# First expert block's rows by matrix products instead of through DRAM, and the turning of the rows ahead of the down product, in one inference step of a four-layer mixture-of-experts trunk

## What is computed

```
def moe(h, w_router, router_bias, w_gate, w_up, w_down):
    s = sigmoid(h @ w_router)                  # 16 experts in 4 groups
    sb = s + router_bias
    ...                                        # best group, then the top 2 experts inside it
    gates = sum(one_hot(idx) * w)              # w: the two scores, normalised to sum 1
    a = einsum('bsd,edf->bsef', h, w_gate)     # d = 1024, f = 256
    u = einsum('bsd,edf->bsef', h, w_up)
    act = silu(a) * u * gates
    return einsum('bsef,efd->bsd', act, w_down)
```

## Time and profile before

| what | value |
|---|---|
| device time, median of 3 runs | 1914.86 us (1914.83 to 1915.51) |
| device time of the profiled execution | 1910.18 us |
| span of the profiled execution on the trace | 1908.4 us |
| PE busy | 1479.9 us (78% of the span) |
| DVE, ACT, POOL busy | 26%, 20%, 12% of the span |
| mean granted clock of PE | 0.911 of full speed |
| bytes moved by DMA | 446.88 MB, mean 234 GB/s |

### The profile page before, as it was taken

The page is one execution under the profiler, slowest core; times in us unless marked ns, Lnnn a source line. Parts: engine busy times, 40 slices in busy tenths (PEclk is TensorE's granted clock), DMA queues, the critical chain, the costliest instruction groups (busy, mean ns, idle before and its releaser), DMA issues.

```text
span 1908.4 us, 26946 instructions
## 1 busy us (share of the span) xinstructions
PE 1479.9 (78%) x11269; PEld 900.8 (47%) x11269; DVE 496.5 (26%) x1105; ACT 385.2 (20%) x983; POOL 234.0 (12%) x296
## 2 busy tenths in 40 slices
PE   2999975997495893899378989849983988849990
PEld 1776752333384672333174456623332766733330
DVE  0126321111326513111223342221113055131113
ACT  1115221111212602111111342201112035011111
POOL 1030012000115012000101000110002030210001
PEclk8999997999698997999789999979996999969995
DMA  9696265998476064699828213649985740538963
GB/s 351 254 327 164 81 256 197 392 415 320 179 257 180 7 243 171 246 419 379 304 90 288 66 45 111 270 157 391 412 324 204 250 118 1 208 145 326 420 280 121
DMA packets 129282, 446.88 MB, mean 234 GB/s; under 512 B 13011, under 2 KB 54822, under 8 KB 104582
## 3 DMA queue, kind: packets, MB, share of 16 engines
q1 hardware_dynamic: 97206, 351.37, 48.8%
q0 software_dynamic: 25152, 89.96, 13.6%
q10 hardware_dynamic: 6800, 3.78, 0.6%
HBM read 395.38 MB, written 49.69 MB: 233 GB/s over the span
## 4 chain that ended last, share of the span: by engine, by line
PE 71%; DVE 10%; issue 7%; DMA 6%; ACT 3%; POOL 1%; SPq 0%; POOLq 0%; DVEq 0%; ACTq 0%
PE bank L1395 62%; PE bank L1693 3%; DMA y_slots<-kT 3%; PE bank L1545 3%; PE bank L1451 2%; DVE pp L1311 2%; DMA xn<-y_slots,row_of 2%; DMA ring<-in_w_mod 1%; DVE xn L1016 1%; ACT pp L898 1%; POOL small L581 1%; DVE V L1372 1%; DVE V L1374 1%; DVE x L1375 1%; PE bank L1589 1%
## 5 line engine op out<-in xcount | busy, mean ns | idle before, releaser
L1395 PE MATMUL bank<-ring,pp 128*32 128x512 f32 x2784 | 417.0, 595 | 17.3 <-DVE pp L1311 14.6
L1395 PE MATMUL bank<-work,pp 128*32 128x512 f32 x1056 | 280.2, 598 | 8.3 <-DVE pp L1311 8.3
L1395 PE MATMUL bank<-ring,hT 128*128 128x256 f32 (+3 forms) x1142 | 262.7, 390 | 6.9 <-DVE hT L1027 3.2
L1395 PEld LDWEIGHTS bank<-ring,hT 128*128 128x128 f32 x1142 | 208.2, 191 | 59.3 <-issue 27.1
L1395 PEld LDWEIGHTS bank<-ring,pp 128*32 128x32 f32 x2784 | 126.8, 110 | 171.7 <-issue 171.7
L1395 PE MATMUL bank<-ring,xn 128*128 128x256 f32 x768 | 169.2, 381 | 0.0
L1395 PE MATMUL bank<-V,pp 128*32 128x512 f32 x768 | 148.8, 619 | 12.3 <-DVE pp L1311 12.3
L1395 PEld LDWEIGHTS bank<-ring,xn 128*128 128x128 f32 x768 | 144.8, 190 | 23.0 <-issue 3.7
L1451 PE MATMUL bank<-ident,xn 128*128 128x128 f32 x192 | 39.5, 397 | 130.3 <-DVE xn L1016 130.3
L1327 DVE TENSOR_TENSOR pp<-bank,pp 128x256 f32<-128x256 f32 x48 | 20.4, 425 | 398.9 <-ACT pp L970 398.9
L1395 PEld LDWEIGHTS bank<-work,pp 128*32 128x32 f32 x1056 | 76.6, 111 | 86.1 <-issue 86.1
(11 more groups left out here) (216 smaller groups left out, 1524.3 us busy)
## 6 DMA issues: line engine op xcount, KB each, us to landing
ring<-in_w_mod SPq DMA_DIRECT2D x96, 1024.0 KB, 9.1
ring<-in_moe_w_down SPq DMA_DIRECT2D x52, 1024.0 KB, 14.4
ring<-in_moe_w_gate SPq DMA_DIRECT2D x32, 1024.0 KB, 16.6
ring<-in_moe_w_up SPq DMA_DIRECT2D x32, 1024.0 KB, 8.5
hT<-h_slots POOLq DMA_DIRECT2D x48, 512.0 KB, 11.1
y_slots<-kT POOLq DMA_DIRECT2D x48, 512.0 KB, 8.3
V<-in_moe_w_gate SPq DMA_DIRECT2D x16, 1024.0 KB, 8.8
V<-in_moe_w_up SPq DMA_DIRECT2D x16, 1024.0 KB, 12.1
```

The source lines that it names most:

```text
L1395: return pe.matmul(out, lhsT, rhs, start=start, stop=stop)
```

## The change

A new constant `slot_no` holds the numbers 0 to 127 on every partition; it is an eighteenth small load. Behind `row_of`, DVE builds `first_of`, three 128x128 matrices of zeros and ones, which lie in a part of `kT` that is not yet in use: element (token, slot) is 1 if either of the token's two slot numbers is that slot. It takes three comparisons and three compare-and-adds. PE multiplies the rows `xn` with them in `gather_rows` (24 float32 products of 128 columns, which is 48 records) and so makes the turned rows of block 0 directly in banks 6 and 7; the copies out of the banks are as before. The scatter to `h_slots` stays, all six DMAs of it; the read of block 0 from the table goes, and the reads of blocks 1 and 2 need wait for nothing but the scatter. In PE's stream `turn_rows(blk + 1)` moves in front of `block_down(blk - 1)`, and in those of ACT and DVE the copies of turned rows move in front of the copies of the down product. The placement of the adaLN products between the output projections is as it was.

The core of the diff, without the lines of constants and semaphores:

```
                 def block_in(blk):
-                    if blk >= 2:
+                    if blk > 2:
                         pool.wait_ge(xT_full, BLOCKS * L + blk - 1)
...
-                block_in(0)
                 block_in(1)
...
                 V_.tensor_copy(row_of[:, :, :], row_f[:, :, :]).then_inc(rows_ready, 1)
+                for b in range(NB):
+                    last = V_.tensor_scalar(first_of[:, b, :], slot_no[:, :], row_f[:, 0, b:b + 1], None, ALU.is_equal)
+                link(last)
+                for b in range(NB):
+                    last = V_.scalar_tensor_tensor(out=first_of[:, b, :], in0=slot_no[:, :],
+                                                   scalar=row_f[:, 1, b:b + 1], in1=first_of[:, b, :],
+                                                   op0=ALU.is_equal, op1=ALU.add)
+                last.then_inc(first_ready, 1)
...
+                def gather_rows(n):
+                    pe.wait_ge(first_ready, L + 1)
+                    pe.wait_ge(xT_a, n + 1)
+                    pe.wait_ge(xT_v, n + 1)
+                    wait_evacuated(pe, *[("hrow", L, b, half) for b in range(NB) for half in range(2)])
+                    for k in range(KC):
+                        for b in range(NB):
+                            ins = mm(bank[6 + k // 4][:, k % 4 * P:(k % 4 + 1) * P], xn[:, b, k::KC],
+                                     first_of[:, b, :], b == 0, b == NB - 1)
+                    ins.then_inc(xT_full, 1)
...
-                turn_rows(BLOCKS * L, 0, 16 * (BLOCKS // 2 * L + 1))
+                gather_rows(BLOCKS * L)
                 for blk in range(BLOCKS):
                     n, slot = BLOCKS * L + blk, blk % 2
                     block_gate_up(blk)
+                    if blk < BLOCKS - 1:
+                        turn_rows(n + 1, 1 - slot, loaded(blk + 1))
                     if blk > 0:
                         block_down(blk - 1)
-                    if blk < BLOCKS - 1:
-                        turn_rows(n + 1, 1 - slot, 16 * (BLOCKS // 2 * L + (blk + 1) // 2 + 1))
```

More of the change, by code:

```diff
@@ L60, in host_constants @@
                rope32=rope(32).reshape(P, 64), first=first,
-               before=r < c, quarters=r % 32 == np.arange(E)[None], ebase=np.tile(SLOTS * np.arange(E)[None], (P, 1)),
+               before=r < c, slot_no=np.tile(np.arange(P)[None], (P, 1)), quarters=r % 32 == np.arange(E)[None], ebase=np.tile(SLOTS * np.arange(E)[None], (P, 1)),
                ebeyond=np.tile(E * SLOTS + (FURTHER - SLOTS) * np.arange(E)[None] - SLOTS, (P, 1)),
@@ L244, in build @@
         quarters = sb("quarters", [P, E])
+        slot_no = sb("slot_no", [P, P])
         rbias = sb("rbias", [P, E])
@@ L326, in build @@
              "r_copied"))
-        lat_sq, lat_rstd, states, wr_ready = (sem(s) for s in ("lat_sq", "lat_rstd", "states", "wr_ready"))
+        lat_sq, lat_rstd, states, wr_ready, first_ready = (sem(s) for s in ("lat_sq", "lat_rstd", "states", "wr_ready", "first_ready"))
         freed = {"v": freed_v, "a": freed_a, "p": probs, "w": wo_mul}
@@ L970, in _ @@
                     nc.scalar.activation(sil[:, slot, :], bank[slot][:, 0:DE], ACT.Silu).then_inc(sil_full, 1)
+                    if blk < BLOCKS - 1:
+                        turned_rows(n + 1, 1 - slot)
                     if blk > 0:
                         first_half(blk - 1)
-                    if blk < BLOCKS - 1:
-                        turned_rows(n + 1, 1 - slot)
                     turn_act(act, n, slot)
@@ L1035, in _ @@
                 free(V_.tensor_copy(dst, src.rearrange("p (c k) -> p c k", c=2) if n == 16 else src))
-            dve.wait_ge(const_in, 16 * 17)
+            dve.wait_ge(const_in, 16 * 18)
             for w in range(2):
@@ L1435, in _ @@
             mods([("mod", 0, v, q) for v in range(2) for q in range(4)])
-            pe.wait_ge(const_in, 16 * 17)
+            pe.wait_ge(const_in, 16 * 18)
             def mod_columns(L, s):
@@ L1754, in block_down, with loaded @@
                     ins.then_inc(y_full, 1)
[L1756 removed]
+                def loaded(blk):
+                    return 16 * (BLOCKS // 2 * L + blk // 2 + 1 if blk % 2 else (BLOCKS // 2 - 1) * L + blk // 2)
+                def gather_rows(n):
[9 more added lines that the diff above has]
+                gather_rows(BLOCKS * L)
                 for blk in range(BLOCKS):
```

5 lines of the change are left out of this document (3 added, 2 removed).

## The result

| what | before | after |
|---|---|---|
| device time, median (4 runs each) | 1914.84 us (1912.26 to 1915.51) | 1868.84 us (1865.95 to 1870.13) |
| ratio, with its 95% interval | | 0.976 (0.9743 to 0.9777) |
| profiled execution, its span | 1910.18, 1908.4 us | 1865.95, 1864.2 us |
| mean granted clock of PE | 0.911 | 0.927 |

The change made the kernel 46.0 us faster. The forecast was 70 us faster, 1845 us, and the range ended at 1860: the direction was right, the size was not, and the time lies 9 us outside the range. In the two profiled executions the difference is 44.2 us of span.

The account below looks back on a forecast made before the run. The prediction took PE to set the pace, with the transfers having almost no room. Four layers saving 10.2 us at the mixture's start and 7.3 in the blocks made 70 us, giving 1845 us, range 1828 to 1860.

Parts of the forecast that it names:

- near block 9: Late in a mixture stage: one PE wait of 1 to 2 us for a weight transfer, once the period is 11.7 us.
- The forecast's balance: Expert 13's weights at gate-up 9: 5.8 - 7.0 + 1.1 - 1.4 = -1.5 us, so PE waits 1.5 us a stage.
- the transfers set every block: Rival, blocks: transfers hold the period at 12.6 us, only the starts' 41 us remain, 1874 us; chance 0.09.
- the read of block 1: Start of each mixture: issued 12.7 us after PE's last count, landing at 16.3, before the first gate-up ends at 18.0.
- gather 7.9 us: Start of each mixture: 48 records, 19.5 in 4.4 us at low clock, the rest in 3.5; bounds 6.0 and 10.8.
- a gather above 11 us: Sign at the start of each mixture that would show the forecast wrong; about 8 us was expected.
- With the clock up: First gate-up product of each mixture: 7.1 us with its tail, instead of 9.0, after the gather.
- first_ready: Start of each mixture: DVE's six instructions take 1.5 us, so it comes 2.0 us after PE's last count.
- The same instructions remain: Blocks: PE's 10.43 + 1.00 + 0.25 = 11.7 us a period without wait, 0.88 less than 12.58.
- The serial gather: Rival, start of each mixture: a record's load and product do not overlap, gather 13.3 us, 1867 us; chance 0.04.
- The late clock: Rival, start of each mixture: clock stays down through the gather, saving 7.3 us there, 58 in all, 1856; chance 0.11.
- No rows came late: Refers to the slower rival, blocks: late reads stop turning and down product, landing after 19.7 us, 1921 us; chance 0.03.

Follow-up runs that it names:

- run 12: Not a run label: in "the blocks, which now run 12 us earlier", "run" is a verb and 12 us a time.

## Why a record of the gather costs 0.244 us

The forecast took the price from weight loads of 128x128 that stood in a row, 0.125 us at full clock and 0.225 at half. Those loads read neighbouring columns. The gather's stationary operand is `xn[:, b, k::KC]`, every eighth float, 32 bytes apart. The next experiments change how these 128 columns lie. The prices of single records below are distances between the starts of neighbouring records in the trace, layer 0.

**Neighbouring columns.** The edit multiplies other columns of `xn` (the result is another one); count, shapes and order of the records stay.

```diff
-                            ins = mm(bank[6 + k // 4][:, k % 4 * P:(k % 4 + 1) * P], xn[:, b, k::KC],
+                            ins = mm(bank[6 + k // 4][:, k % 4 * P:(k % 4 + 1) * P], xn[:, b, k * P:(k + 1) * P],
```

> The changed kernel, but gather_rows reads 128 neighbouring columns of xn as its stationary operand instead of every eighth column. Leaves out the right choice of columns: block 0 then multiplies the wrong 128 features with each part of the weights, with the same instructions and sizes. Theory A (the strided read of float32 weights sets the 0.244 us a record): the gather takes 6.0 to 8.5 us instead of 11.7, first gate-up product ends 3 to 5.5 us earlier in each layer, 1847 to 1857 us in all. Theory B (load and product of a record simply follow one another, or three accumulations into one place do): 11.7 us as before and 1869 us.

Measured: 1852.05 us (1851.4 to 1853.37), ratio 0.9692 (0.9676 to 0.9708). The gather takes 8.10, 8.15, 8.55 and 7.27 us in the four layers; the forecast was 7.9. Chain of layer 0, then three stretches of its gather, columns as above:

```profile
290.08 8.10 PE bank L1404 x48
...
299.14 7.11 PE bank L1404 x64
```

```profile
291.00:295.00 4.00, 4.00 (x21) 4.00 (x20) 1.83 (x10) 0.00 (x0) 3.08 (x4) 0.50 0.91 360
294.00:295.00 1.00, 1.00 (x7) 1.00 (x6) 0.00 (x0) 0.00 (x0) 0.69 (x2) 0.50 0.99 401
296.00:298.00 2.00, 2.00 (x20) 1.97 (x18) 0.00 (x0) 0.00 (x0) 0.94 (x1) 1.00 0.96 377
```

Here the records do follow the clock: they start 0.213 us apart at half clock and 0.111 at full, where those of the changed kernel start 0.240 and 0.238 apart. So the stride costs 0.03 us a record while the clock is low and 0.13 once it is up: what it takes away is the gain from the clock.

**Steps of 8 and of 16 bytes**, to see where the price begins:

```diff
-                            ins = mm(bank[6 + k // 4][:, k % 4 * P:(k % 4 + 1) * P], xn[:, b, k::KC],
+                            ins = mm(bank[6 + k // 4][:, k % 4 * P:(k % 4 + 1) * P], xn[:, b, k % 4 * 2 * P:(k % 4 + 1) * 2 * P:2],
...
-                            ins = mm(bank[6 + k // 4][:, k % 4 * P:(k % 4 + 1) * P], xn[:, b, k::KC],
+                            ins = mm(bank[6 + k // 4][:, k % 4 * P:(k % 4 + 1) * P], xn[:, b, k % 2 * 4 * P:(k % 2 + 1) * 4 * P:4],
```

> The changed kernel, but gather_rows reads every second column of xn as its stationary operand, not every eighth; block 0 then multiplies the wrong 128 features with each part of the weights. Theory A (any step between the columns of a float32 product's weights doubles their read): 0.244 us a record, 11.7 us, as with a step of eight. Theory B (the price grows with the step, or comes from where the eight-fold step lands in memory): a gather between 8 and 11 us.

> The changed kernel, but gather_rows reads every fourth column of xn as its stationary operand (16 bytes apart; eight-fold steps are 32 bytes, two-fold 8); block 0 then multiplies the wrong 128 features with each part of the weights. With steps of one and two the gather took 8.1 to 8.3 us in layer 0, with eight 11.73 whatever the clock. Theory A (the price grows with the distance): 9 to 10.5 us in layer 0. Theory B (there is a bound at 32 bytes): 7.3 to 8.5. Theory C (the bound lies at 16): 11.7.

Measured, one run each: 1853.43 us with step two, and gathers of 8.18, 8.29, 7.29 and 7.59 us; 1869.48 us with step four, and 11.45 us in every layer. The chains of both, step two first:

```profile
290.40 8.18 PE bank L1404 x48
```

```profile
291.81 11.45 PE bank L1404 x48
```

| step, bytes | a record at half clock, us | at full clock, us | gather, layer 0, us |
|---|---|---|---|
| 4 | 0.213 | 0.111 | 8.10 |
| 8 | 0.213 | 0.118 | 8.18 |
| 16 | 0.233 | 0.233 | 11.45 |
| 32 | 0.240 | 0.238 | 11.73 |

Every second float is all but free, every fourth costs nearly what every eighth does, whatever the clock. These four steps fit a price that depends on how many of the floats read lie in 16 bytes: with two or more it is hardly seen, with one the read sets the pace. They don't tell this from a bound on the step itself between 8 and 16 bytes. The Trainium skill states such a rule ("Advanced Engine Details and Errata", section "Memory Cachelines"): the buffer has lines of 16 bytes and wants at least two hits on one. The runs agree with it. The Trainium skill ("SBUF — State Buffer", the note on cachelines in the section "Door 1: The DMA port swizzle") puts the free stride at four floats; step four at 11.45 us against 8.18 speaks against this, and the measurement decides. Why 32 bytes cost a little more than 16, and 8 a little more than 4, stays open.

**The same product from rows that are stored permuted.** The float of index 8j + k is put at 128k + j when the rows are copied out of PSUM, so that the gather and the transposes read neighbours and nothing else is computed. The copies now write with a step of 512 bytes.

```diff
-                return xn[:, key[2], key[3] * 512:(key[3] + 1) * 512], ps[:, :]
+                return (xn[:, key[2], :].rearrange("p (k j) -> p j k", k=KC)[:, key[3] * 64:(key[3] + 1) * 64, :],
+                        ps[:, :].rearrange("p (j k) -> p j k", k=KC))
...
-                                           xg[:, slot, k::KC], ident[:, :])
+                                           xg[:, slot, k * P:(k + 1) * P], ident[:, :])
...
-                            ins = mm(bank[6 + k // 4][:, k % 4 * P:(k % 4 + 1) * P], xn[:, b, k::KC],
+                            ins = mm(bank[6 + k // 4][:, k % 4 * P:(k % 4 + 1) * P], xn[:, b, k * P:(k + 1) * P],
```

> The changed kernel with the features of every row stored in another order (8 j + k at place 128 k + j), so that gather_rows and turn_rows read neighbouring columns; the copies of hrow out of PSUM write in steps of 512 bytes instead. Same result. Theory A (the strided read of float32 weights is the gather's cost): the gather takes 7.3 to 8.6 us, as in the run with neighbouring columns, and the time is within 4 us of that run's 1852. If the strided writes of the six hrow copies cost more than the reads gain, the copies (0.59 and 0.69 us now) take well over 1 us each and PE's last count comes later by up to 3 us a layer: over 1860. The transposes, 0.125 us each with a stride, should not change by more than 0.02 each.

Measured: 1853.52 us (1850.03 to 1859.58), ratio 0.9688 (0.9671 to 0.9704), gathers of 8.56, 7.72, 8.28 and 8.46 us. The copy of the rows in the timeline of the changed kernel, and then in this one:

```profile
276.04 0.69 DVE L1012 COPY xn<-bank 128x512 f32<-128x512 f32 x1 [2.87 <-PE bank L1668]
```

```profile
277.33 1.04 DVE L1013 COPY xn<-bank 128x512 f32<-128x512 f32 x1 [2.91 <-PE bank L1669]
```

The scattered write costs 0.35 us a copy on DVE (and 0.47 on ACT), ahead of a gather that is some 3.5 us shorter. Against the kernel before in its own set of runs, this kernel is 58.2 us faster and the one with neighbouring columns 58.7, the changed kernel 46.0 and 42.7. So what neighbouring columns give, some 12 to 16 us, can be had without computing something else.

**The clock's share.** In the third layer the first gate-up took 8.75 us, not 7.11. The stretch 1239 to 1241 of the changed kernel:

```profile
1239.00:1241.00 2.00, 2.00 (x12) 0.46 (x8) 0.00 (x0) 0.00 (x0) 0.54 (x1) 0.50 0.93 297
```

The clock was back at 1.2 GHz there, although PE had been busy for the 11.7 us of the gather up to a pause of 1 us for the copies. Of the 28 stages in the seven profiled runs with a gather of 11.4 us or more, 9 had a first gate-up of 8.6 to 8.8 us; of the 20 stages in the five runs with a gather of 7.1 to 8.6 us none had. In three of those 20 the clock fell one pause later instead, ahead of the second gate-up (8.7 to 8.8 us where 7.07 is usual). In all nine the clock had risen 5.47 to 6.23 us after the gather began, in the other 19 at most 5.45 or at least 6.50 us after; so when it rises has to do with whether it falls again. Why it falls in one stage and not in the next was not settled.

## Why the period is 12.10 us and not 11.7

The sum of the forecast was 10.43 + 1.00 + 0.25. The rows after read 7.00 + 3.57 = 10.57 for the same products, 1.09 for the eight transposes and 0.44 for the two. Before, gate-up and down ran into each other and the two transposes stood in front of a wait; now products and transposes change places four times in a period instead of twice. Two experiments take the added changes back in different ways, and the 0.75 us wait does not return.

**All transposes in a row**, ahead of the down product. ACT's copy of the turned activations moves ahead of its copy of the down product too; PE's stream:

```diff
                     if blk < BLOCKS - 1:
                         turn_rows(n + 1, 1 - slot, loaded(blk + 1))
-                    if blk > 0:
-                        block_down(blk - 1)
                     pe.wait_ge(act_full, n + 3)
                     pe.wait_ge(acT_ready, n + 1)
                     turn_gated(act_sb[:, slot, :]).then_inc(acT_full, 1)
+                    if blk > 0:
+                        block_down(blk - 1)
```

> The changed kernel with the two transposes of the gated activations moved right behind the eight of the rows, ahead of the down product. Theory A (changes between products and transposes cost 0.13 us each): two changes fewer in a period, 11.8 to 11.9 us instead of 12.10, 4 x 10 x 0.25 = 10 us less, 1858 to 1860. Theory B (the transfers hold the period near 12.1, or bring waits once the period is shorter): the period on PE shows waits for weights and the time is 1864 to 1869. If SiLU and DVE's product are not done when the eight transposes end, PE waits 0.1 to 0.4 us a period for DVE and the gain is half or less.

Measured: 1872.81 us (1870.07 to 1878.39), ratio 0.9797 (0.978 to 0.9813). The timeline of PE shows why it gives nothing: its 96 records of products take 10.48 us (10.57 in the changed kernel), but SiLU and DVE's product have only the eight transposes as cover, and PE stands 0.20 us for them; the last block, which turns no rows, has no cover at all, and PE stands 1.30 us. The blocks of a stage take 135.1 us instead of 132.9.

```profile
369.92 1.16 PE L1702 MATMUL bank<-ident,hT 128*128 128x128 f32 x8
371.29 0.51 PE L1714 MATMUL bank<-ident,pp 128*128 128x128 f32 x2 [0.20 <-DVE pp L1336]
...
444.08 0.51 PE L1714 MATMUL bank<-ident,pp 128*128 128x128 f32 x2 [1.30 <-DVE pp L1336]
```

**All transposes in a row, in the middle of the down product**, whose first half then covers SiLU. ACT's copy of the turned activations moves as in the experiment before; of `block_down`, which now takes the halves it is to do, only the calls are shown:

```diff
                     block_gate_up(blk)
+                    if blk > 0:
+                        block_down(blk - 1, (0,))
                     if blk < BLOCKS - 1:
                         turn_rows(n + 1, 1 - slot, loaded(blk + 1))
-                    if blk > 0:
-                        block_down(blk - 1)
...
                     turn_gated(act_sb[:, slot, :]).then_inc(acT_full, 1)
+                    if blk > 0:
+                        block_down(blk - 1, (1,))
```

> The changed kernel with both groups of transposes between the two halves of the down product, so that one half stands directly behind the gate-up product and the other directly ahead of the next. Theory A (a change between products and transposes costs PE some 0.13 us each, and this leaves two of four): SiLU's result, ready 1.35 us behind the gate-up product, is there before the transposes ask for it, and a period takes 11.8 to 11.9 us; about 10 us less in all, 1857 to 1860. Theory B (the transfers hold the period at 12.1): waits for weights in PE's row, 1865 or more. By my sum of the slack of expert 13 (5.8 us less 8 x 0.73, plus 1.1, less 1.2) it should be used up to within 0.5 us, so waits of up to 1 us a stage near block 9 are possible in A too.

Measured: 1861.37 us (1860.14 to 1862.82), ratio 0.9734 (0.9718 to 0.975). Chain: a period of 348.73 - 336.96 = 11.77 us, and one wait ahead of gate-up 9:

```profile
336.96 10.44 PE bank L1404 x96
...
348.73 10.44 PE bank L1404 x96
...
409.42 1.01 issue
410.43 8.79 PE bank L1404 x80
```

Half down, next gate-up and half down in one run take 10.44, the ten transposes 1.33. So two changes between products and transposes were worth 12.10 - 11.77 = 0.33 us a period, 0.13 of it in the products and 0.2 in the transposes. Why such a change costs PE time was not looked for. The stage as a whole gains less, 131.4 us against 132.9 in layer 0, as PE waits 1.01 us for weights, and at the end of a stage two transposes now stand ahead of the half of the down product that the first store of the tail waits for. The wait that the forecast placed "near block 9" appears once the period is as short as it assumed.

## What the transfers allow

In the changed kernel the up weights of expert 13 (SP's issue in the timeline, and the time to landing in the list of DMAs, us last):

```profile
393.19 0.43 SPq L504 DMA_DIRECT2D work<-in_moe_w_up  x1
...
work<-in_moe_w_up SPq DMA_DIRECT2D x1, 1024.0 KB, 14.3
```

They land at 407.5, and gate-up 9 starts at 409.90: 2.4 us of slack. The forecast's balance, 5.8 - 8 x saving + 1.1 - share taken by rows, gives 5.8 - 8 x 0.48 + 1.1 - 0.8 = 2.3 with the true period.

**Half of the down product left out** in every block, so that PE is too fast for the queue:

```diff
-                    for half in range(2):
+                    for half in range(1):
```

> The changed kernel without the second half of every down product (columns 512 to 1023 of the experts' results are not computed), all transfers as before: it shows what period the transfers allow, since PE alone would need 12.10 - 1.78 = 10.3 us. Theory A (transfers of 5.24 MB a block at 415 to 421 GB/s are the limit just under 12.1): the first blocks run at 10.3 us, then PE waits for weights and the period from block 5 on is 12.3 to 12.6 us; a stage is no more than 5 us shorter than in the changed kernel. Theory B (the transfers were full only because they were asked for at that pace): 10.3 us to the end, 18 us less a stage, 1800 us.

Measured, one run: 1855.60 us. PE's period is 10.38 us (335.86 - 325.47) at first, and then it waits, in the timeline 5.85 us ahead of gate-up 6 and 3.83 us ahead of gate-up 9, at 410.33:

```profile
325.47 7.00 PE bank L1404 x64
...
335.86 7.00 PE bank L1404 x64
```

```profile
372.87 1.07 PE L1404 MATMUL bank<-V,pp 128*32 128x512 f32 x3 [5.85 <-issue]
```

```profile
345.00:434.00 89.00, 79.33 (x644) 27.42 (x640) 13.11 (x22) 13.56 (x30) 6.87 (x13) 0.92 1.01 421
```

From gate-up 6 to gate-up 9 it is 37.46 us, 12.49 a block, at 421 GB/s (the stretch above). The clock is low for a part of this stretch (0.92 in the row), but PE still stands idle ahead of gate-up 9, so this is the pace of the queue. A kernel whose PE needs 1.7 us less in each block has a stage only 4.2 us shorter (128.7 against 132.9, layer 0). The rival "the transfers set every block" was right about the pace (12.6) and wrong about when it rules: ten periods of 12.10 overdraw it by some 4 us, and the slack of 5.8 us and the idle share of block 2 pay for that.

## A faster version

**Both repairs together**, permuted rows and transposes in the middle of the down product.

> Both edits together, same result as the reference's. If they are independent, the sum of their savings: some 17 + 10 us under the changed kernel, 1842 us. If the blocks, which now run 12 us earlier against the weights' first release only in their own pace, hit the transfers, the second saving is halved: 1847.

Measured: 1848.32 us (1845.61 to 1854.36), ratio 0.9674 (0.9652 to 0.9696). Gathers of 7.64, 7.07, 8.28 and 7.07 us; chain of the blocks:

```profile
333.73 10.44 PE bank L1405 x96
...
405.76 1.63 issue
407.39 8.79 PE bank L1405 x80
```

The period is 11.70 us, and PE waits 1.63 us a stage for weights: the forecast's two numbers for the blocks, 11.7 and 1.5, on a kernel that has the period it assumed.

**One more step**: an activation of one element on ACT behind the first copy of turned rows, so that SiLU's table is loaded while PE runs the first gate-up.

```diff
                 turned_rows(BLOCKS * L, 0)
+                nc.scalar.activation(warm[:, :], x[:, 0, 0:1], ACT.Silu)
```

> The fastest kernel so far (rows stored in the other order, transposes between the halves of the down product) with one more instruction on ACT, a SiLU of one element behind the copy of block 0's turned rows, so that the load of the SiLU table (1.28 us) falls under the first gate-up product and not behind it. Theory A (the gap of 3.15 us from the first gate-up to the second is ruled by that load, SiLU, the product with it and the copy): the gap falls to 1.9 us, 4 x 1.28 = 5 us less, 1843. Rival: the copy out of PSUM needs the table changed back, or the read of block 1, which lands shortly ahead of the end of the first gate-up, is late, and the gap falls by less than 0.5 us: 1848.

Measured: 1846.08 us (1844.34 to 1847.84), ratio 0.9658 (0.9642 to 0.9674). The table load lies beside the gate-up, and the second gate-up starts 1.97 us after the end of the first, where it was 3.15:

```profile
299.48 7.11 PE bank L1407 x64
...
306.76 0.40 ACT pp L974
...
308.56 8.79 PE bank L1407 x80
```

```profile
299.10 1.28 ACT L966 ACT_TABLE_LOAD   x1
```

The step should bring 4 x 1.18 = 4.7 us; the medians differ by 2.2 and the intervals overlap, since in the profiled execution the gathers took 2.0 us more in sum, with the clock coming up later, and PE waited 1.5 us longer for weights in the last layer. That it is the faster of the two is likely and not shown; that both beat the changed kernel (0.976) is.

## Where the prediction was right and wrong

**Wrong, the price of a gather record.** The term "gather 7.9 us" was worked out from loads of neighbouring columns, and its bounds, 6.0 and 10.8, both follow the clock. The stationary operand's step of 32 bytes, which stands in the code, was not weighed. It makes 11.7 us: 3.8 us a layer, 15.2 in all, more than half of the error. With neighbouring columns the same working holds within 0.2 us in layer 0 (8.10; the clock rose after 5.2 us, where 4.4 was assumed, and a record took 0.213 and 0.111 us, not 0.225 and 0.125). So the price of such a record and the late rise of the clock were about right, and the access pattern was what the term left out. The forecast named "a gather above 11 us" as what would show it wrong, and so it did.

**Wrong, the first gate-up in one layer.** "With the clock up" held in three of four layers, the fourth gives 1.6 us back.

**Close, the rest of the start.** `first_ready` 2.3 us after the last count (2.0 forecast), the copies 0.96 (1.0), the gate-up 7.11 (7.1), the read of block 1 at 13.7 (12.7) and never waited for, the gap of 3.15 unchanged. The 0.25 in `first_ready` (2.23 to 2.28) makes 1.0 over four layers. 15.2 + 1.6 + 1.0 = 17.8 of the 18.1 us by which 22.7 falls short of 40.8; the other 0.3 is the kernel before, whose four starts are 28.1 us in the mean, not 28.2.

**Wrong, the period.** "The same instructions remain" is true of their number, not of their time: 10.57, 1.09 and 0.44 instead of 10.43, 1.00 and 0.25. That is 0.4 us a period, 4.0 us a stage. The two last transposes stand in rows 5 with 0.40 us, not 0.25, only that there the wait for DVE that was to go hid their end. The two added changes between products and transposes were put at nothing.

**Right, the balance of the transfers**, although its wait of 1.5 us did not come: at 12.10 us it gives 2.3 us of slack (2.4 measured). At 11.77, 5.8 - 8 x 0.81 + 1.1 - 1.3 gives 0.9 us of wait (1.01 measured in layer 0 of the split version, 0.61 to 1.30 in the others), and at 11.70 it gives 1.5 (1.56 to 1.72). So the blocks lost 4.0 and got back 1.5 of it: 2.5 a stage, 10 in all, against 29.2 - 19.4 = 9.8 measured.

**The rivals.** The serial gather gave 1867, which is nearly the time measured, by coincidence. It asked for 0.44 us a record at half clock, and the trace has 0.240 there; its 0.235 at full clock is met by chance, since with neighbouring columns the records take 0.213 and 0.111, load beside product. Its gather was 1.6 us a layer too long (13.3 against 11.7), which stood in for part of the 2.5 us a layer that the blocks did not give. The late clock explains nothing of the 11.7 us, since the records took the same with the clock at 0.50 and at 1.00; the clock rose 3.7 to 6.5 us after the gather's start, and the gather took 11.71 to 11.73 us in all four layers. No rows came late, and the eighteenth load left no trace.

## What to carry to other kernels

A price read from a row holds for the access pattern of that row: before it goes into a sum, compare the step in bytes of the operand in both places, not only the shape. When a wait is removed, look at what ran into it; the last instruction ahead of the wait has part of its length hidden in it, and it comes back. For work that draws on a full queue, keep the slack as an account (slack, less what each period now asks for, plus idle shares): in layer 0 it gave the slack or the wait within 0.15 us in three kernels.

## What was not expected of the hardware

- A product with 128 columns of float32 as weights: the records start 0.233 us apart with a step of 16 bytes and 0.24 with 32, at either clock; with a step of 4 or 8 bytes 0.213 at 1.2 GHz and 0.11 to 0.12 at 2.4 GHz.
- The transposes hardly pay for the same step: eight take 1.09 us with 32 bytes and 1.02 in the permuted version. The cause was not looked for.
- A change from products of 32 rows side by side to full transposes and back costs in sum some 0.33 us beyond the two already there.
- The granted clock fell to 1.2 GHz behind a gather in which the profile shows PE busy throughout, in 9 of 28 stages.
- Copies of 128x512 floats out of PSUM that write with a step of 512 bytes take 1.04 us on DVE and 1.06 on ACT, against 0.69 and 0.59.
